# Two attentions inside a fused trunk layer: how the softmax weights are turned, and where gate products stand in a step

## What is computed

```python
# h = RMSNorm(x); proj = h @ w_in, cut into latents, q/k/v, the state-space input and the gate logits
def causal_block_attention(q, k, v, log_forget_cum=None):
    for i in range(seq // 128):                 # blocks of 128 queries, keys up to the block's end
        s = einsum('bqhd,bkhd->bhqk', qb, kb) * scale      # (+ c_q - c_k in attention B)
        p = softmax(where(mask, s, -1e30)); out_i = einsum('bhqk,bkhd->bqhd', p, vb)
# A: multi-head latent attention ("MLA"), 4 heads of 96, B: forgetting attention ("FOX"), 4 heads of 64,
# C: a state-space branch ("S5"); 1024 tokens, width 1024
gates = sigmoid(gate_logits)                    # 3 x 1024 columns of proj
x = x + (sum_i gates_i * (branch_i @ w_branch_i)) @ w_out
x = x + conv_gated_ffn(RMSNorm(x))              # inner width 2816
```

## Time and profile before

| | |
|---|---|
| median of 3 runs | 1408.11 us (1408.01 to 1408.66) |
| the profiled execution | 1408.35 us, its span 1406.6 us |
| TensorE busy | 99% of the span |
| VectorE, ScalarE, GpSimd busy | 74%, 49%, 12% |
| granted clock | 1.00 of full speed |

### The profile page before, as it was taken

The page is one execution under the profiler, slowest core; times in us unless marked ns, Lnnn a source line. Parts: engine busy times, 40 slices in busy tenths (PEclk is TensorE's granted clock), DMA queues, the critical chain, the costliest instruction groups (busy, mean ns, idle before and its releaser), DMA issues.

```text
span 1406.6 us, 19078 instructions
## 1 busy us (share of the span) xinstructions
PE 1396.8 (99%) x6986; PEld 1166.7 (83%) x6986; DVE 1038.2 (74%) x1527; ACT 684.6 (49%) x1111; POOL 165.4 (12%) x174
## 2 busy tenths in 40 slices
PE   9999999999999999999999999999999999999999
PEld 7988888888788888878888888888888888888887
DVE  6888666656876657769545888778877777588886
ACT  6344356656555431266323755555555555434332
POOL 2002511103361021123000100000000000000000
PEclk9999999999999999999999999999999999999999
DMA  7022211241121223277622222222222224890222
GB/s 266 30 84 69 76 53 61 66 136 38 55 61 40 83 76 91 77 247 253 239 92 75 60 90 90 72 78 90 90 75 90 87 64 147 316 386 4 97 75 82
DMA packets 131111, 149.99 MB, mean 107 GB/s; under 512 B 11402, under 2 KB 93245, under 8 KB 130621
## 3 DMA queue, kind: packets, MB, share of 16 engines
q1 hardware_dynamic: 130832, 148.72, 32.1%
q10 hardware_dynamic: 189, 0.08, 0.0%
HBM read 111.88 MB, written 36.31 MB: 105 GB/s over the span
## 4 chain that ended last, share of the span: by engine, by line
PE 97%; DVE 1%; ACT 1%; DMA 1%; issue 0%; SPq 0%; POOL 0%; ACTq 0%
PE ps L2566 30%; PE ps L945 18%; PE ps L2875 5%; PE ps L2876 5%; PE ps L2877 5%; PE ps L2966 4%; PE ps L1152 3%; PE ps L3528 2%; PE ps L3530 2%; PE ps L3529 2%; PE ps L1129 2%; PE ps L482 2%; PE ps L484 2%; PE ps L483 2%; PE ps L1848 2%; PE ps L443 1%
## 5 line engine op out<-in xcount | busy, mean ns | idle before, releaser
L2566 PE MATMUL ps<-split_arena 128*128 128x512 f32 x1320 | 306.4, 389 | 0.8 <-ACT up_part L2451 0.8
L2566 PEld LDWEIGHTS ps<-split_arena 128*128 128x128 f32 x1320 | 247.6, 188 | 52.6 <-issue 1.2
L945 PE MATMUL ps<-split_arena 128*128 128x512 f32 x1152 | 290.3, 399 | 0.5 <-ACT plain_arena L980 0.4
L945 PEld LDWEIGHTS ps<-split_arena 128*128 128x128 f32 x1152 | 208.6, 188 | 41.5 <-issue 1.5
L2749 ACT ACTIVATE down_ops<-down_all 128x1024 fp32r<-128x1024 f32 x77 | 81.5, 1061 | 114.9 <-PE ps L2877 112.9
L2768 DVE TENSOR_TENSOR down_ops<-down_all,down_ops 128x1024 fp32r<-128x1024 f32 x77 | 94.0, 1221 | 45.7 <-ACT down_ops L2749 45.6
L2566 PE MATMUL ps<-up_b,split_arena 128*128 128x512 f32 x528 | 127.0, 389 | 0.0
L2875 PE MATMUL ps<-down_ops 128*128 128x512 f32 x308 | 119.9, 389 | 0.0
L2876 PE MATMUL ps<-down_ops 128*128 128x512 f32 x308 | 119.8, 389 | 0.0
L2877 PE MATMUL ps<-down_ops 128*128 128x512 f32 x308 | 119.8, 389 | 0.0
L2566 PEld LDWEIGHTS ps<-up_b,split_arena 128*128 128x128 f32 x528 | 99.0, 188 | 20.5
(11 more groups left out here) (452 smaller groups left out, 2598.3 us busy)
## 6 DMA issues: line engine op xcount, KB each, us to landing
plain_arena<-in_w_in SPq DMA_DIRECT2D x26, 512.0 KB, 4.0
scr_gate<-plain_arena SPq DMA_DIRECT2D x48, 256.0 KB, 2.0
plain_arena<-scr_gate SPq DMA_DIRECT2D x24, 512.0 KB, 4.5
plain_arena<-in_w_up SPq DMA_DIRECT2D x22, 512.0 KB, 5.2
up_raw<-in_w_up SPq DMA_DIRECT2D x22, 512.0 KB, 4.8
scr_act<-plain_arena SPq DMA_DIRECT2D x22, 512.0 KB, 2.6
down_all<-scr_act SPq DMA_DIRECT2D x18, 512.0 KB, 9.7
down_all<-in_w_down SPq DMA_DIRECT2D x18, 512.0 KB, 10.8
```

The costliest lines, as they stand in the source:

```text
L945: mm = nc.tensor.matmul(m.ps[:, self.banks[half], :], w[:, k, :], src[:, k, h * BANK:(h + 1) * BANK], start=(j == 0), stop=(j == self.PER_ ...
L2566: mm = nc.tensor.matmul(o, self.w[j][w][:, k, :], self.h[j][k][h], start=(j in self.OPENS and k == 0 and n == 0), stop=(k == self.HK - 1 a ...
```

## The change

Nothing is computed otherwise. Four things are edited.

1. **Halves.** In steps with five to eight key tiles (`i` of 4 to 7) the weights are turned as upper and lower 64 rows: for each tile one transpose of 64x128 into bank 4 or 5 and one into the other, with a 64x64 identity. The two fills of the step are now "64 queries by all tiles" each, and both are turned in one run (`turn_halves`), which waits until both banks are empty. ScalarE and VectorE read two fills of up to 512 columns (64 times the number of tiles).
2. **Low halves first.** In those steps VectorE takes the low halves of step `s - 1` before `norm(s)` and no longer after it.
3. **Three counts a step.** The gate products of a step are dealt as ahead (after the scores), between runs (after q or k is turned and before the wait for the scaled weights) and behind (after the weights). The number per head is unchanged (72; in the first heads 110 in FOX and 92 in MLA).
4. **Values first.** In even steps with halves, `values` comes ahead of `behind`.

FOX's later heads have, for `i` of 3 to 7, before (0,5) (0,4) (0,6) (9,6) (8,10), after (0,0,4) (0,0,2) (0,6,0) (6,6,5) (2,7,10). MLA's later heads have after (0,0,6) (0,0,4) (0,6,0) (7,7,0) (3,7,8).

```diff
-LATER_HEAD = [(0, 8), (0, 8), (2, 6), (0, 5), (0, 4), (0, 6), (9, 6), (8, 10)]
-LAST_HEAD = [(0, 8), (0, 8), (2, 6), (0, 4), (0, 6), (0, 4), (10, 4), (12, 8)]
-FOX_FILL = [(14, 9), (4, 11), (2, 10), (0, 12), (0, 10), (0, 6), (8, 6), (8, 10)] + LATER_HEAD * (H - 2) + LAST_HEAD
-MLA_FILL = [(12, 8), (8, 4), (2, 10), (0, 6), (0, 4), (0, 6), (8, 6), (10, 8)] + LATER_HEAD * (H - 2) + LAST_HEAD
+HEAD_START = [(0, 0, 8), (0, 0, 8), (2, 0, 6)]
+LAST_HEAD = HEAD_START + [(0, 0, 4), (0, 0, 6), (0, 0, 4), (10, 0, 4), (12, 0, 8)]
+FOX_LATER = HEAD_START + [(0, 0, 4), (0, 0, 2), (0, 6, 0), (6, 6, 5), (2, 7, 10)]
+MLA_LATER = HEAD_START + [(0, 0, 6), (0, 0, 4), (0, 6, 0), (7, 7, 0), (3, 7, 8)]
+FOX_FILL = ([(14, 0, 9), (4, 0, 11), (2, 0, 10), (0, 0, 12), (0, 0, 4), (0, 7, 0), (6, 7, 6), (2, 7, 9)]
+            + FOX_LATER * (H - 2) + LAST_HEAD)
+MLA_FILL = ([(12, 0, 8), (8, 0, 4), (2, 0, 10), (0, 0, 6), (0, 0, 4), (0, 6, 0), (7, 7, 0), (3, 7, 8)]
+            + MLA_LATER * (H - 2) + LAST_HEAD)
...
+    @staticmethod
+    def in_halves(s):
+
+        return s % TT >= 4
+
+    def turn_halves(self, pe, f):
+
+        _, s, _, n = self.fills[f]
+        pe.wait_ge(self.lo, f)
+        for j in range(n):
+            for e in range(2):
+                r, bank = slice(64 * e, 64 * e + 64), 4 + (f + e) % 2
+                tr = self.m.nc.tensor.transpose(self.m.ps[:, bank, 64 * j:64 * j + 64], self.p_buf[s % 2][r, j * P:(j + 1) * P], self.m.ident[r, r])
+                if j == n - 1:
+                    tr.then_inc(self.turned, 1)
...
             for f in self.qk_fills(s):
                 self.turn(pe, f)
+            self.fill.tensor(pe, between_runs)
             pe.wait_ge(self.normed, s + 1)
-            *first, last = self.fills_of("p", s)
-            for f in first:
-                self.turn(pe, f)
-
-            if first:
-                self.fill.tensor(pe, behind)
-            self.turn(pe, last)
-            if not first:
-                self.fill.tensor(pe, behind)
-            if s >= 2 and s % 2 == 0:
+            first, *second = self.fills_of("p", s)
+            if second:
+                self.turn_halves(pe, first)
+            else:
+                self.turn(pe, first)
+            values_first = second and s % 2 == 0
+            if values_first:
+                self.values(pe, s // 2 - 1)
+            self.fill.tensor(pe, behind)
+            if s >= 2 and s % 2 == 0 and not values_first:
                 self.values(pe, s // 2 - 1)
...
-            _, s, a, n = x
-            slot = self.kept_at(s % TT)
-            return [self.pt[e][:, a:a + n, slot, :] for e in range(2)], self.m.ps[:, 4 + f % 2, 0:n * P].rearrange("p (j q) -> p j q", q=P)
+            _, s, e, n = x
+            slot, q = self.kept_at(s % TT), P // 2 if self.in_halves(s) else P
+            return [p[:, 0:n, slot, q * e:q * e + q] for p in self.pt], self.m.ps[:, 4 + f % 2, 0:n * q].rearrange("p (j q) -> p j q", q=q)
...
+            self.fill.scalar(act, between_runs)
+            self.fill.copy_made(act)
+            for f in self.fills_of("p", s):
                 self.split_hi(act, f)
-            if first:
-                self.fill.scalar(act, behind)
-                self.fill.copy_made(act)
-            self.split_hi(act, last)
-            if not first:
-                self.fill.scalar(act, behind)
+            self.fill.scalar(act, behind)
...
+            lows_first = s < ATT_STEPS and self.in_halves(s)
+            if lows_first:
+                for f in self.fills_of("p", s - 1):
+                    self.split_lo(dve, f)
             if s < ATT_STEPS:
                 self.norm(dve, s)
             if i == 7 and not last:
                 self.maximum(dve, s + 1)
-            if s:
+            if s and not lows_first:
                 for f in self.fills_of("p", s - 1):
                     self.split_lo(dve, f)
```

More of the change, by code:

```diff
@@ L1056, in __init__ @@
             fills += self.turned_in(s)
-            fills += [("p", s, a, min(4, s % TT + 1 - a)) for a in range(0, s % TT + 1, 4)]
+            fills += [("p", s, e, s % TT + 1) for e in range(2 if self.in_halves(s) else 1)]
         self.fills = fills
@@ L1103, in turn @@
         if x[0] == "p":
-            _, s, a, n = x
+            _, s, _, n = x
             for j in range(n):
-                tr = nc.tensor.transpose(bank[:, j * P:(j + 1) * P], self.p_buf[s % 2][:, (a + j) * P:(a + j + 1) * P], m.ident[:])
+                tr = nc.tensor.transpose(bank[:, j * P:(j + 1) * P], self.p_buf[s % 2][:, j * P:(j + 1) * P], m.ident[:])
         else:
@@ L1165, in tensor @@
             i = s % TT
-            ahead, behind = self.table[s]
+            ahead, between_runs, behind = self.table[s]
             if i == 7 and s + 1 < ATT_STEPS:
@@ L1509, in gpsimd @@
         for s in range(ATT_STEPS):
-            ahead, behind = FOX_FILL[s]
+            ahead, *later_on = FOX_FILL[s]
             made += ahead
@@ L1516, in gpsimd @@
                     att.copy_q(pool, h, half)
-            made += behind
+            made += sum(later_on)
         fill.gpsimd(pool, FOX_UNITS + 1 - fill.split)
```

## The result

The changed kernel takes 1423.90 us (median of four runs, 1423.44 to 1424.80) beside 1408.06 us (1407.89 to 1408.66) on the same chip: 1.0113 times as long, 95% interval 1.0101 to 1.0125. That is 15.8 us slower. The forecast had the side right and the size too small: +9.4 us, with a range that ended at 1422.5.

The account below looks back on a forecast made before the run. It took TensorE, 97% of the chain that ended last, as the bound. Its terms 0.6 + 2.1 + 2.15 + 2.0 + 4.5 - 1.9 gave +9.45 us on the profiled 1408.35: 1417.8, or 1417.5 on the median; range 1407.5 to 1422.5.

Parts of the forecast that it names:

- part 1: Runs of half transposes on TensorE: 0.046 us a tile cheaper, but 0.35 of edges a run; +0.6 us, bounds -9.6 and +1.6.
- parts 2 and 3: At i = 4: TensorE waits for low halves put before the norm, +2.1 us; FOX's norm meets GpSimd, +2.15.
- part 4: At i = 5: the transposes wait for q's low half, 0.35 us idle in six heads; +2.0 us, bounds 0.8 and 3.0.
- part 5: At i = 6: waits for k's low half in FOX and a late half-unit copy in MLA; +4.5 us, bounds 1.5 and 6.
- removed: Waits behind half units' ends that go: 0.5 each in last heads, 0.12 in five heads, 0.3 in FOX's first; -1.9 us.
- move by less: SyncE's stores and loads follow the gate banks' copies and move by less than the forecast times; no term in the sum.
- granted in full: TensorE's clock, taken as granted in full; no term in the sum.
- the norm's meeting with L991: FOX's second head, i = 4: the norm comes behind GpSimd's L991 and ends near 218.0, not 215.9; +2.15 us.
- MLA's tie: MLA's norm asks as L991 starts; left out of the sum, a rival if lost: 3.1 us more, 1420.6 us, 15%.
- 2.12 less 1.83: Part 4's chain to i = 5's last transposes, 2.12 us, against TensorE's work, 1.83; it took 0.35 idle.
- 0.3 in a head and 0.9 in the second: Part 5's idle time on TensorE in FOX at i = 6; it entered the sum as +0.9 in FOX.
- Values and halves after a half unit's end give the copy its time: The reason for the removed waits: work behind a half unit's end covers ScalarE's copy; -1.9 us.

Follow-up runs that it names:

- pool_two: The changed kernel with GpSimd's subtraction L991 as two instructions of half the width each: 1422.33 us.
- norm_first: The changed kernel with VectorE doing the norm ahead of the low halves again in all steps: 1422.07 us.
- low_first_alone: The kernel before with one edit alone, low halves ahead of the norm in steps of five to eight tiles: 1414.18 us.
- mla_8_6: The changed kernel with (8,6,0) for (7,7,0) at the seventh block of MLA's first three heads: 1422.08 us.
- copy_last: The changed kernel with FOX's last completed half unit copied out after the last step, ahead of the output rows: 1421.94 us.
- eighth_old: The changed kernel with the eighth step of each attention's first three heads turned the old way, low halves still first: 1421.63 us.
- kept_busy_two: The changed kernel with ten unread matmuls ahead of TensorE's wait for the norm, in FOX's second head at i = 4: 1422.25 us.
- last_head_only: The kernel before in the first three heads, the changed order in the last, two counts there exchanged, FOX's last copy at its products' end: 1406.59 us.
- whole_tiles: The changed kernel with the five to eight tiles turned whole again, in one run at the same place: 1425.45 us.
- kept_busy: The changed kernel with ten unread matmuls behind TensorE's wait for the norm, in FOX's second head at i = 4: 1426.41 us.
- combo: The changed kernel with MLA's half unit cut 8 and 6, FOX's last copy made earlier and GpSimd's subtraction in two: 1419.32 us.
- combo_eighth: combo with the eighth step of the first three heads turned the old way as well: 1418.80 us.

## Why the prediction was right in its side and short in its size

Waits below are what a distance from start to start has over an undisturbed one; ahead of halves the undisturbed one is that of whole tiles (0.23 us behind a product), since part 1 has what halves and whole tiles differ by.

| step | forecast | measured |
|---|---|---|
| part 1, halves | +0.6 | -1.5 |
| parts 2 and 3, `i = 4` | +4.25 | +4.2 |
| part 4, `i = 5` | +2.0 | +2.2 |
| part 5, `i = 6` | +4.5 | +5.2 |
| removed | -1.9 | -2.5 |
| copy wait at a head's start | not in it | +2.5 |
| ahead of the halves of `i = 7`, and of `i = 6` in the last heads | not in it | +1.5 |
| end of FOX, SyncE's queue | "move by less" | +2.05 |
| clock | "granted in full" | +1.7 |
| sum | +9.45 | +15.35 |

The profiled executions are 15.1 us apart, the medians 15.8. Part 1 is a difference of two medians whose runs overlap, so the sum is good to about 1 us and no better. The 1.5 us are eight waits of 0.19 us: six at `i = 7`, two at `i = 6`.

*Right.* Parts 2 and 3: 2.95 us at FOX's second head, 0.91 at the third, 0.50 at the last, less 0.1 each that was there before in two of them. Taking the norm's meeting with L991 as certain in FOX and leaving MLA's tie out held too: there L991 started 0.09 us after the norm. That rival, with 1420.6 us, did not come about. pool_two, norm_first and low_first_alone confirm the mechanism. Part 4: 0.42 us in each of MLA's first three heads, 0.32 to 0.59 in FOX's, less 0.3 in all that was there before; the prediction's own 2.12 less 1.83 makes 0.29 and not the 0.35 that it took. Part 5: 1.28, 1.36 and 1.28 us at MLA's boundary for 1.0, 1.6 and 1.0, and 0.19, 0.72 and 0.41 in FOX. FOX had +0.9 in the sum, where its own 0.3 in a head and 0.9 in the second come to 1.2 for the second and third alone; 1.3 were measured. mla_8_6 shows the boundary.

*Part 1* was mis-sized. "Where TensorE idles ahead of the run its first edge (0.10) is hidden; that is so in about ten of 32 runs" counted only new waits, and took 0.35 us of edges from S5, where nothing waits. With waits ahead of 20 of the 32 runs the 0.046 us a tile counts for more. The error went the other way from the misses and hid part of them, which was luck for its size. Its side needed no luck: the waits that it named outweigh part 1 with either value.

*Three steps failed.* The first is the step on the copies and stores: "SyncE's stores and loads follow the copies of the gate banks, whose number is unchanged, and move by less than these times". The number is unchanged, but one copy moved by 13.6 us (295.61 to 309.19, of which some 8 are FOX's own delay), past two loads in SyncE's queue. copy_last prices it at 2.0 us.

The second is the step "Values and halves after a half unit's end give the copy its time". It holds at `i = 6`: the waits of the last heads and the five of 0.12 to 0.15 us went, and so did 0.34 us ahead of the last values of each attention, which the prediction did not count. One of the five, in the kernel before (timeline of TensorE, MLA's second head; 0.15 us from the last transpose to the product, 0.03 undisturbed):

```profile
419.56 0.60 PE L1106 MATMUL ps<-ident,plain_arena 128*128 128x128 f32 x4
420.03 1.63 PE L945 MATMUL ps<-split_arena 128*128 128x512 f32 x6
```

It does not hold for the half unit that ends with `i = 7`. There the change takes four transposes out from behind the end, and the copy's wait at the next head's start grows from 0.12 to 0.57 us in three FOX heads and from nothing to 0.39 in three of MLA. I had looked at what stands behind a half unit's end in step 6 and not in step 7. eighth_old prices the step at 2.3 us.

The third is "The clock is granted in full". It was a statement on the kernel before; the sum itself had a hole of about 3 us on TensorE and did not ask what that does to the clock. kept_busy_two prices it at 1.65 us.

By the table the three make 6.25 us of the 6.4 that are missing, and part 1 takes 2.1 of them back. What is left is no single step. The waits of 0.19 us have 1.5, parts 4 and 5 have 0.9 more than forecast, and the medians lie 0.7 further apart than the profiled executions; the 0.6 that more was removed than forecast goes the other way.

The Trainium skill, TensorE: Matmul & The Clock Gate, Part 1, says that the gate sets the clock by how busy the engine has lately been, and calls the moment of the change variable from run to run. By that rule a hole made of a VectorE wait has a second price after it; the traces of the changed kernel and of kept_busy_two agree, with a granted clock of 0.55 and 1.00 in the same 3.2 us.

## What to carry to other kernels

When a wait is moved or a run made longer, follow the first consumer of every bank it touches into the next iteration and the next stage: the two largest misses were a copy that lost its cover one head later and a dropped call that put a DMA load behind a late store. Count a hole in TensorE's stream of two and a half microseconds or more as more than its length, and fill it even with useless work if its end can't be moved. A run of transposes that needs two banks empty belongs where no other split on VectorE stands ahead of them: in last_head_only it has no wait at `i = 4`, in FOX's second head of the changed kernel 2.95 us.

## What the runs showed of the hardware that was not expected

- After 2.6 to 2.8 us idle the granted clock fell in every profile that has such a hole (changed kernel, whole_tiles, low_first_alone, eighth_old, kept_busy, mla_8_6, copy_last), in one ahead of the hole's end (low_first_alone) and in the others 0.5 to 1.8 us after TensorE had resumed. After 1.7 us idle at this place it fell in one profile of three (combo 0.61 at 219 to 222 us; pool_two and combo_eighth 1.00). The 1.65 to 1.69 us ahead of MLA's transposes (L1862) left it at 1.00 in all eight profiles that have them, the 2.12 us in S5 of combo_eighth too, and so did every hole of 1.2 us or less. The fall may make the scatter too: whole_tiles gave 1423.61 us with a mean clock of 1.000 and 1425.4 to 1425.7 in its three runs at 0.999, while kept_busy_two and last_head_only, at 1.000 throughout, spread over 0.9 and 0.8 us.
- A VectorE norm (SBUF to SBUF, one input) that asks behind a GpSimd subtraction waits for the instruction under way and not for the next in GpSimd's list: 2.59 us behind one of 2.34, 1.52 behind the first of two. The Trainium skill, SBUF — State Buffer, section on the two sides, gives the shared pair to whoever starts first for a whole instruction; the traces agree, and two shorter GpSimd instructions took 1.07 us off the norm.
- Half transposes pay only their second edge where a wait precedes them: the distance from the last one to the next matmul is 0.15 us in every run of the changed kernel's attentions, with or without a wait, while the distance from a product to the first half is 0.32 us and from a product to a whole tile 0.23.
